# Ten seven-product quads per column pair instead of eight, in three runs of three, and the latents kept in DRAM earlier

## What is computed

```
h = layer_norm(x, emb_ln_g, emb_ln_b)
proj = h @ w_in[l]                     # 256 x 4096 by 4096 x 22592
q_a, kv_a, dq, dk, dv, g_mla, g_dswa, r_mla, r_dswa = jnp.split(proj, IN_OFFSETS, axis=-1)
a = mla_attention(q_a, kv_a, ...)      # latent queries q_a (1024), latent keys kv_a (512 + 64)
b = dilated_mixture(dq, dk, dv, rel_bias)
merged = jax.nn.sigmoid(r_mla) * y_mla + jax.nn.sigmoid(r_dswa) * y_dswa
out = merged @ w_out[l]
h = layer_norm(DEEPNORM_ALPHA * h + out, ln_g[l], ln_b[l])
```

## Time and profile before

| | |
|---|---|
| time, median of 3 runs | 2697.34 us (2696.78 to 2700.26) |
| time of the profiled execution | 2698.62 us |
| its span, first to last instruction | 2696.8 us |
| PE busy | 2652.6 us (98%) |
| DVE busy | 1996.6 us (74%) |
| ACT busy | 1321.1 us (49%) |
| POOL busy | 248.0 us (9%) |
| moved by DMA | 606.36 MB, mean 225 GB/s |
| column pairs | from about 174 us to about 1575 us |

### The profile page before, as it was taken

One profiled execution on the slowest core, in us unless ns is written; L12 is line 12 of the kernel. 1 busy time (PEld: TensorE's weight loads), 2 busy tenths in 40 slices (PEclk: granted clock), 3 DMA queues, 4 the chain that ended last, 5 costly groups with the idle time before them and its releaser, 6 DMA issues.

```text
span 2696.8 us, 32780 instructions
## 1 busy us (share of the span) xinstructions
PE 2652.6 (98%) x12351; PEld 2215.3 (82%) x12351; DVE 1996.6 (74%) x1913; ACT 1321.1 (49%) x1277; POOL 248.0 (9%) x349
## 2 busy tenths in 40 slices
PE   7998999999999999999999999999999999999998
PEld 5977888888888888888888889988888888888886
DVE  7757888888888888888888867775565576656557
ACT  5434555555555555555555555554444444433333
POOL 0000111011111011111011101111010100100000
PEclk9999999999999999999999999999999999999998
DMA  6667888788877888877888864357776767776765
GB/s 204 180 226 222 250 245 243 233 244 255 248 243 239 246 246 244 250 246 234 246 244 249 251 194 141 125 155 214 243 236 178 237 219 237 247 231 224 230 217 176
DMA packets 237098, 606.36 MB, mean 225 GB/s; under 512 B 17161, under 2 KB 33909, under 8 KB 236708
## 3 DMA queue, kind: packets, MB, share of 16 engines
q1 hardware_dynamic: 198992, 506.51, 57.4%
q0 software_dynamic: 36752, 95.61, 15.3%
q10 hardware_dynamic: 1224, 2.44, 0.2%
HBM read 577.16 MB, written 27.34 MB: 224 GB/s over the span
## 4 chain that ended last, share of the span: by engine, by line
PE 95%; DVE 2%; DMA 2%; issue 0%; ACT 0%; SPq 0%; DVEq 0%; ACTq 0%
PE acc L606 13%; PE acc L608 13%; PE acc L607 13%; PE bank L626 4%; PE bank L630 4%; PE bank L631 4%; PE acc L631 4%; PE acc L626 4%; PE acc L630 4%; PE acc L665 2%; PE acc L669 2%; PE acc L668 2%; PE bank L665 2%; PE bank L668 2%; PE acc L614 2%; PE acc L613 2%
## 5 line engine op out<-in xcount | busy, mean ns | idle before, releaser
L1017 ACT ACTIVATE q_hi<-q_raw 128x2048 fp32r<-128x2048 f32 x272 | 522.0, 1920 | 611.7 <-PE bank L631 187.5
L1220 DVE TENSOR_TENSOR w_lo<-w_raw,w_hi 128x1024 fp32r<-128x1024 f32 (+2 forms) x448 | 504.6, 1139 | 293.8 <-ACT w_hi L976 289.5
L1303 DVE TENSOR_TENSOR q_low<-q_raw,q_hi 128x2048 fp32r<-128x2048 f32 x272 | 620.1, 2285 | 39.4 <-ACT q_hi L1017 39.4
L976 ACT ACTIVATE w_hi<-w_raw 128x1024 fp32r<-128x1024 f32 (+2 forms) x448 | 431.6, 982 | 299.3 <-PE acc L608 256.0
L606 PE MATMUL acc<-w_hi,oper_hi 128*128 128x512 f32 (+1 forms) x1072 | 410.4, 383 | 1.6 <-DVE w_lo L1220 1.6
L608 PE MATMUL acc<-w_hi,oper_lo 128*128 128x512 f32 (+1 forms) x1072 | 405.7, 378 | 0.0
L607 PE MATMUL acc<-w_lo,oper_hi 128*128 128x512 f32 (+1 forms) x1072 | 405.3, 378 | 0.0
L1307 DVE TENSOR_TENSOR q_sum_low<-q_sum,q_hi 128x1536 fp32r<-128x1536 f32 x136 | 238.0, 1750 | 0.0
L606 PEld LDWEIGHTS acc<-w_hi,oper_hi 128*128 128x128 f32 x1072 | 201.3, 188 | 39.4 <-DVE w_lo L1220 3.0
L1823 POOL DMA_DIRECT2D q_raw<-in_w_in x136 | 117.8, 866 | 1244.9 <-DMA q_raw<-in_w_in 1244.9
L608 PEld LDWEIGHTS acc<-w_hi,oper_lo 128*128 128x128 f32 x1072 | 201.2, 188 | 37.6
(11 more groups left out here) (347 smaller groups left out, 4588.1 us busy)
## 6 DMA issues: line engine op xcount, KB each, us to landing
q_raw<-in_w_in SPq DMA_DIRECT2D x256, 1024.0 KB, 5.7
w_raw<-in_w_in SPq DMA_DIRECT2D x128, 512.0 KB, 4.6
w_raw<-in_w_out SPq DMA_DIRECT2D x128, 512.0 KB, 3.9
q_raw<-in_w_in POOLq DMA_DIRECT2D x136, 256.0 KB, 5.8
w_raw<-in_w_o_mla SPq DMA_DIRECT2D x64, 512.0 KB, 5.0
q_raw<-in_w_in SPq DMA_DIRECT2D x32, 512.0 KB, 4.8
w_raw<-in_w_o_dswa SPq DMA_DIRECT2D x32, 512.0 KB, 4.4
w_raw<-in_w_q_b SPq DMA_DIRECT2D x32, 384.0 KB, 3.6
```

The source lines that it names most:

```text
L976: act.activation(w_hi[:, n % RING, 0:w], w_raw[:, n % RING, 0:w], ACT.Copy).then_inc(w_hi_ready, 1)
L1017: act.activation(q_hi[h][:, 0:4, :], q_raw[r][:, :, :], ACT.Copy).then_inc(q_hi_ready, 1)
L1220: dve.tensor_tensor(w_lo[:, n % RING, 0:w], w_raw[:, n % RING, 0:w], w_hi[:, n % RING, 0:w].bitcast(F32), ALU.subtract).then_inc(w_lo_read ...
L1303: dve.tensor_tensor(q_low[r], q_raw[r], q_hi[h][:, 0:4, :].bitcast(F32), ALU.subtract).then_inc(q_lo_ready, 1)
```

## The change

`SEVEN` gets ten members, in three runs of three after a single one. The token sums get two more entries, at other slots of `start`; their buffers grow by 8 KB. To make room, `q_raw[2]` moves to where the latent keys `kva_hi` and `kva_lo` lie, so these are stored to DRAM (`kva_d`) before the pairs and loaded again behind them. The first half of the latent queries is stored early, the second half once it is there. For the first pair, `sums_late` holds at q = 1 and no longer never, and the copy of the second half of the latent queries (g = 1) stands ahead of the sums. `store_pair` is now issued at q = 8 (it was q = 9). Buffers are renumbered in the order in which they come free.

```
-SEVEN = (2, 4, 5, 7, 9, 11, 13, 14)
+SEVEN = (2, 4, 5, 6, 8, 9, 10, 12, 13, 14)
-QA_RAW = RAWS - 1
+KVA_RAW, QA_RAW = 2, RAWS - 1
-T_STEPS = (("qa0", 5), ("qa0", 8), ("qa0", 11), ("qa0", 14), ("kva0", 4), ("kva0", 8), ("kva0", 12), ("kva1", 12))
+T_STEPS = (("qa0", 5), ("qa0", 8), ("qa0", 11), ("qa0", 14), ("kva0", 3), ("kva0", 6), ("kva0", 9), ("kva0", 12), ("kva1", 10), ("kva1", 13))
+    kva_d = nc.dram_tensor("latent_keys", (P, 2, KV_RANK // P, SEQ), F32).ap()
...
     # SP, quad_loads
-                    elif g in (2, 3):
-                        sp.wait_ge(slot_done, SEC["start"].per_slot - (2 if g == 2 else 0))
+                    elif g == KVA_RAW:
+                        sp.wait_ge(kva_stored, 32)
+                    elif g in (3, 4):
+                        sp.wait_ge(slot_done, SEC["start"].per_slot - (2 if g == 3 else 0))
                     elif g == QA_RAW:
-                        sp.wait_ge(qa_stored, 16)
+                        sp.wait_ge(qa_stored, 32)
...
     # PE, ahead of unit0
+                            pe.wait_ge(kva_loaded, 32)
...
     # DVE, column_pairs
-                    sums_late = p > 0 and q == SEVEN[0] + 1
+                    sums_late = q == SEVEN[0] + 1 if p else q == 1
                     if g + 1 < NQ and is_seven(g + 1) and not sums_late:
                         quad_sums(g + 1)
                     if p and q == 2:
                         direct_out(p - 1)
                     quad_low(g)
-                    if sums_late:
+                    if g == 1:
+                        dve.wait_ge(slot_done, SEC["start"].per_slot)
+                        dve.tensor_copy(qa_sb[:, :, CW:2 * CW], acc[1][:, :, :]).then_inc(acc_free, 1)
+                    if sums_late and is_seven(g + 1):
                         quad_sums(g + 1)
                     if p and q == 0:
                         mixed_out(p - 1)
-                    if g == 1:
-                        dve.wait_ge(slot_done, SEC["start"].per_slot)
-                        dve.tensor_copy(qa_sb[:, :, CW:2 * CW], acc[1][:, :, :]).then_inc(acc_free, 1)
...
     # POOL
+            pool.wait_ge(acc_free, 1)
+            pool.dma_start(qa_d[:, :, 0:CW], qa_sb[:, :, 0:CW]).then_inc(qa_stored, 16)
+            pool.wait_ge(nT_lo, KV_RANK // P)
+            pool.dma_start(kva_d[:, 0, :, :], kva_hi[:, :, :].bitcast(F32)).then_inc(kva_stored, 16)
+            pool.dma_start(kva_d[:, 1, :, :], kva_lo[:, :, :].bitcast(F32)).then_inc(kva_stored, 16)
             for g in range(NQ):
                 if is_seven(g):
                     first_sum(g)
                 if g == SEVEN[0]:
                     pool.wait_ge(acc_free, 4)
-                    pool.dma_start(qa_d[:, :, :], qa_sb[:, :, :]).then_inc(qa_stored, 16)
+                    pool.dma_start(qa_d[:, :, CW:2 * CW], qa_sb[:, :, CW:2 * CW]).then_inc(qa_stored, 16)
                 if g >= QUADS and g % QUADS == SEVEN[4]:
                     store_pair(g // QUADS - 1)
...
```

More of the change, by code:

```diff
@@ L315, in program @@
         R_A = RINGS + 48 * K
-        R_B = R_A + 36 * K
+        R_B = R_A + 44 * K
         R_C = R_B + 16 * K
-        R_D = R_C + 32 * K
-        SMALL = R_D + 8 * K
+        SMALL = R_C + 32 * K
         def sb(name, at_, shape, dt=F32):
@@ L336, in program @@
         t_hi = sb("t_hi", R_A, [P, len(SEVEN), 4, P], F32R)
[L337 to L341, removed]
+        t_lo = sb("t_lo", R_A + 2 * len(SEVEN) * K, [P, len(SEVEN), 4, P], F32R)
+        h_pair = sb("h_pair", R_A + 4 * len(SEVEN) * K, [P, 2, SEQ])
+        t_val = sb("t_val", R_A + (4 * len(SEVEN) + 2) * K, [P, 4, P])
+        q_raw = [sb(f"q_raw{n}", at_, [P, 4, CW]) for n, at_ in enumerate((R_B, R_B + 8 * K, R_C + 16 * K, RINGS + 32 * K, RINGS + 40 * K, R_C + 24 * K))]
+        q_low = [sb(f"q_low{n}", at_, [P, 4, CW], F32R) for n, at_ in enumerate((R_B, R_B + 8 * K, R_C + 16 * K, RINGS + 32 * K, RINGS + 40 * K, R_C + 24 * K))]
         q_hi = [sb(f"q_hi{n}", at_, [P, 7, CW], F32R) for n, at_ in enumerate((R_C, RINGS, RINGS + 14 * K))]
@@ L344, in program @@
         q_sum_low = [sb(f"q_sum_low{n}", SMALL + 3328 + n * 6 * K, [P, 3, CW], F32R) for n in range(2)]
-        c_first = sb("c_first", R_A + 32 * K, [P, 2, CW])
+        c_first = sb("c_first", R_A + 4 * len(SEVEN) * K, [P, 2, CW])
         c_sb = [c_first[:, 0, :], c_first[:, 1, :], sb("c_third", R_C + 14 * K, [P, CW]), sb("c_fourth", RINGS + 28 * K, [P, CW])]
@@ L464, in program @@
         q_loaded = [sem(f"q_loaded{n}") for n in range(RAWS)]
-        qa_stored, qa_loaded = sem("qa_stored"), sem("qa_loaded")
+        qa_stored, qa_loaded, kva_stored, kva_loaded = (sem(n) for n in ("qa_stored", "qa_loaded", "kva_stored", "kva_loaded"))
         s1_made = [sem(f"s1_made{n}") for n in range(RAWS)]
@@ L1839, in _ @@
                     pool.wait_ge(acc_free, 4)
-                    pool.dma_start(qa_d[:, :, :], qa_sb[:, :, :]).then_inc(qa_stored, 16)
+                    pool.dma_start(qa_d[:, :, CW:2 * CW], qa_sb[:, :, CW:2 * CW]).then_inc(qa_stored, 16)
                 if g >= QUADS and g % QUADS == SEVEN[4]:
                     store_pair(g // QUADS - 1)
-            last_user = NQ - 1 - (NQ - 1 - QA_RAW) % RAWS
-            pool.wait_ge(raw_free, last_user - last_user // QUADS)
-            pool.dma_start(qa_sb[:, :, :], qa_d[:, :, :]).then_inc(qa_loaded, 16)
+            for buffer in (KVA_RAW, QA_RAW):
+                last_user = NQ - 1 - (NQ - 1 - buffer) % RAWS
+                pool.wait_ge(raw_free, last_user - last_user // QUADS)
+                if buffer == QA_RAW:
+                    pool.dma_start(qa_sb[:, :, :], qa_d[:, :, :]).then_inc(qa_loaded, 16)
+                else:
+                    pool.dma_start(kva_hi[:, :, :].bitcast(F32), kva_d[:, 0, :, :]).then_inc(kva_loaded, 16)
+                    pool.dma_start(kva_lo[:, :, :].bitcast(F32), kva_d[:, 1, :, :]).then_inc(kva_loaded, 16)
             store_pair(PAIRS - 1)
```

## The result

The changed kernel takes 3042.53 us (median of 4 runs, 3040.6 to 3044.45) against 2697.25 us in the same job. The ratio is 1.1277, with a 95% interval of 1.1258 to 1.1297: 345 us slower. The forecast was 2961 us with a range of 2884 to 3010. The direction and the place were right, and the size was short by 81.5 us.

A forecast was written before the change was run, and what follows sets the result against it. PE's matmuls were taken to fill the whole 81.6 us pair. From 2698.6 us, +208.4 (gaps net of matmuls saved), +66 (clock) and -11 (start) gave 2962, with the median 1.3 lower: 2961 us, range 2884 to 3010.

The forecast's parts named there:

- What bounds the kernel: In the pairs, PE's 360 matmuls fill the whole 81.6 us period; any wait of PE lengthens the kernel by as much.
- The wait between two neighbours: At quads 5, 9, 13, PE stops until DVE has done the next sums and low part: 51 gaps, +231.5 us.
- The start: At the start of the pairs, the chain moves up and the first gap goes; -11 us, bounds 0 and -20.
- Matmuls removed: Per pair, two more seven-product quads save 1.36 us of matmuls; 23.1 us less over 17 pairs.
- The clock: After the 51 new PE gaps, the clock falls in most, 1.3 us each: +66 us (0 to 102).
- The rival of the dearest clock: Clock drops at all 51 gaps, costing 1.66 to 2.0 us each: 2980 to 2997 us; chance 0.15.
- What costs nothing: Token sums in `start` 0 to +3 us, keys' stores and reloads 0 to +2; added accumulations and moved addresses nothing.
- The faster rival: DVE's order in the pairs costs nothing and only matmuls count: 2663 us; chance 0.04.

The follow-up runs named there:

- old list in new frame: Changed kernel with the earlier list of eight seven-product quads and its eight token-sum steps; 2688.53 us, ratio 0.9958.
- five-place order: Changed kernel with VectorE making the low part before the next quad's sums at q = 5, 7, 9, 11, 13; 2670.19 us, ratio 0.989.
- gaps filled: Changed kernel with 17 zero-block matmuls on PE ahead of the low-part wait at q = 5, 9, 13; 2906.34 us, ratio 1.0767.

## Why the prediction was right or wrong, point by point

The runs split the 345 us by differences of medians. Three of the four come from one job; the last compares two jobs, whose kernels before lay 1.8 us apart.

| step | forecast | measured | from |
|---|---|---|---|
| latents sooner, the start's order | -11 | -10.5 | old list in new frame - before |
| 102 matmuls fewer | -23.1 | -18.3 | five-place order - old list in new frame |
| the gaps themselves, 51 | +231.5 | +236.2 | gaps filled - five-place order |
| the lower clock, 51 gaps | +66 | +136.2 | changed kernel - gaps filled |

- **What bounds the kernel** was right. Every stop of PE came out in the time, even those of 0.8 us.
- **The wait between two neighbours** was right in place, number and size: gaps at quads 5, 9 and 13, ended by low(5), low(9), low(13), 4.31 us of idle where 4.3 was worked out. Undoing the order removes them, and putting a run of three into the old kernel makes them.
- **The start** was right: quad 4 began at 203.19 and not 212.57, against "near 202". PE reached it at 198.16, 3 us later than I had it, so the gap there was shorter than forecast.
- **Matmuls removed** was 4.8 us too much. In the five-place order a pair takes 80.41 us where 354 matmuls make 80.24, which is 3 us of it over 17 pairs; DVE is at 190 of 200 us there, and low(6) is ready at 376.41, only 0.15 us before PE starts quad 6. Nearly all of the rest is the two added token sums, which the prediction put at nothing (0 to +3 us): ahead of the pairs PE waits for `w_lo` 2.9 us in 5 places with ten token-sum steps, and 1.2 us in 2 places with eight, in the kernel before and in the old list in the new frame alike. That is 1.7 us.
- **The clock** is the step that failed: the term of +66 us measured 136.2, and these 70 of the 81.5 us are nearly the whole error. That the clock would fall was right, but it fell at all 51 gaps where I had four in five; that is 51 x 1.66 - 66 = 18.7 us of the error. The other 51.5 us are the price of one gap, 2.67 us and not 1.66, which I had taken from the gap of 6.57 us at the start of before. The low level lasts 6.8 us there too (182.5 to 189.3), but PE had stood still until 185.98: half of the low stretch cost nothing. In the gap of 4.3 us at 413.63 the clock falls 3.1 us in, and 5.6 us of it fall on matmuls, worth half of that, 2.8. Over all 51 gaps it was 5.9 us on average, worth 2.9; why the runs show 0.3 less isn't settled, though a slower quad also gives DVE time that it doesn't have behind a filled gap. I took the shorter gap to be the milder case, with 2.0 as its upper bound; it is the dearer one. Behind the 8.67 us gap the low level lasted longer, from 206.4 to 216.6, but only 4.0 us of it fell on matmuls (from 212.57), near the 1.96 that I read there. Two readings of the prediction were also 0.2 us late: by the windows of the earlier trace rows the clock fell 3.1 and 2.5 us after PE stopped and not 3.3 and 2.7. In the changed kernel it fell as late as 3.7 us in, which is still inside the 4.31.
- **The rival of the dearest clock.** The rule of the Trainium skill that I had as a rival ("TensorE: Matmul & The Clock Gate", section on HAM oscillation: every tile begins slow) is what happened. The trace agrees at 50 of the 51 gaps, where the clock was down before PE went on at 4.31 us; at the first it fell 0.3 us after. But I priced that rival with 1.66 to 2.0 a gap and so put it at 2980 to 2997.
- **What costs nothing** held for the reload of the keys and the added transfers, which don't show, and not for the two token sums, as above.

The faster rival (only matmuls count) was wrong for this kernel, and is what the five-place order makes of it: 2670 us against the 2663 that I gave it.

## What to carry to other kernels

Where an engine's order is written by hand, go through it for each new neighbourhood and ask what stands behind each wait: a wait for a buffer that is harmless two steps ahead of its use becomes a stop of the bounding engine when the step in between goes. When PE will stop, price the clock by how much of the low stretch falls on matmuls after the stop, not by the loss seen behind a longer gap. And when a change that removes work comes out slower, look for an order that pays before giving it up: here two of DVE's steps exchanged at five places turned +12.8% into -1.1%.

## What the runs showed of the hardware that I had not expected

- A stop of 2.5 us can be enough for TensorE's clock to fall, and the fall can come after PE has gone on (1.2 us after, at 457.3), so a gap that looks harmless is paid for in the quad behind it. It did so at 19 of 51 such gaps; which ones and why stays open.
- Behind stops of 4.3 us the low level lasted 6.8 us, whether they came every 27 us (50 of 51 gaps) or every 89 us (16 of 17), and 3.4 us at the first such gap of either kernel; behind stops of 2.5 us it lasted 3.4 us, behind the one of 8.67 us 10.2 us.
- Matmuls with a zero stationary block hold the clock: 17 of them in each gap saved 136 us without changing the result.
- A stop of PE cost a little more than its length: behind a stop of 0.83 us the next 8 matmuls took 1.95 us and not 1.81, with the granted clock at its upper level.
